# Prompt and decode attention of a hybrid decoder step, run as two stages or as one

## What is computed

```python
def fox_attention(q, k, v, cq, ck, q_pos, k_pos):
    scale = Dh ** -0.5
    ...
        s = jnp.einsum('bqhd,bkhd->bhqk', qi, k).astype(F32) * scale
        s = s + ci[..., None] - ckt[:, :, None, :]
        s = jnp.where(k_pos[None, :] <= pi[:, None], s, MASK_VALUE)
        p = jax.nn.softmax(s, axis=-1).astype(v.dtype)
        return jnp.einsum('bhqk,bkhd->bqhd', p, v)
```

## Time and profile before

| what | us |
|---|---|
| median of three executions | 1936.76 |
| the profiled execution's own time | 1939.86 |
| its span in the profile | 1938.0 |
| TensorE busy in it | 1837.7 |
| last matmul ahead of the attention stages, start | 1021.20 |
| first score of prompt attention, start | 1032.59 |
| first transpose of decode attention, start | 1124.99 |
| first instruction of the next stage (ACT, L1765), start | 1448.45 |

### The profile page before, as it was taken

One profiled execution on the slowest core, in us unless ns is written; L12 is line 12 of the kernel. 1 busy time (PEld: TensorE's weight loads), 2 busy tenths in 40 slices (PEclk: granted clock), 3 DMA queues, 4 the chain that ended last, 5 costly groups with the idle time before them and its releaser, 6 DMA issues. The chain is left out here.

```text
span 1938.0 us, 39358 instructions
## 1 busy us (share of the span) xinstructions
PE 1837.7 (95%) x16353; PEld 1689.5 (87%) x16353; DVE 924.7 (48%) x1392; ACT 692.5 (36%) x1082; POOL 581.1 (30%) x283
## 2 busy tenths in 40 slices
PE   6999998999999999999997999888979999999998
PEld 5999997999999999999995766555559999999998
DVE  4757766345555511156546854343433555555000
ACT  5365454431222212156525754343333322222111
POOL 2333332233333343334325500000003333334332
PEclk9999998999999999999997999999999999999999
DMA  5232241222232323242434799999984222223322
GB/s 120 79 101 79 79 110 40 77 87 87 78 88 77 96 80 86 71 140 55 121 93 112 238 357 380 405 406 407 407 306 122 88 77 88 79 86 89 90 76 79
DMA packets 291653, 277.82 MB, mean 143 GB/s; under 512 B 20114, under 2 KB 250611, under 8 KB 290964
## 3 DMA queue, kind: packets, MB, share of 16 engines
q1 hardware_dynamic: 289540, 272.82, 43.0%
q10 hardware_dynamic: 1792, 1.44, 0.3%
q0 software_dynamic: 144, 1.05, 0.1%
HBM read 254.64 MB, written 16.43 MB: 140 GB/s over the span
## 5 line engine op out<-in xcount | busy, mean ns | idle before, releaser
L2046 POOL TENSOR_TENSOR a_wl<-a_wraw,a_wh 128x1024 fp32r<-128x1024 f32 (+2 forms) x91 | 233.3, 2565 | 394.8 <-ACT a_wh L1970 394.8
L2046 POOL TENSOR_TENSOR b_wl<-b_wraw,b_wh 128x1024 fp32r<-128x1024 f32 (+1 forms) x67 | 175.4, 2618 | 295.1 <-ACT b_wh L1970 295.1
L1927 PE MATMUL ps<-xh,a_wh 128*128 128x288 f32 x1104 | 239.0, 298 | 5.1 <-POOL a_wl L2046 5.1
L1927 PE MATMUL ps<-xl,a_wh 128*128 128x288 f32 x1104 | 237.5, 297 | 0.0
L1927 PE MATMUL ps<-xh,a_wl 128*128 128x288 f32 x1104 | 237.2, 297 | 0.0
L1970 ACT ACTIVATE a_wh<-a_wraw 128x1024 fp32r<-128x1024 f32 (+2 forms) x91 | 100.6, 1105 | 339.5 <-PE ps L1927 324.5
L1970 ACT ACTIVATE b_wh<-b_wraw 128x1024 fp32r<-128x1024 f32 (+1 forms) x67 | 76.0, 1135 | 318.3 <-PE ps L1927 318.3
L1927 PEld LDWEIGHTS ps<-xh,a_wh 128*128 128x128 f32 x1104 | 177.6, 188 | 6.5 <-issue 5.7
L1927 PEld LDWEIGHTS ps<-xh,a_wl 128*128 128x128 f32 x1104 | 177.7, 188 | 0.6
L1927 PEld LDWEIGHTS ps<-xl,a_wh 128*128 128x128 f32 x1104 | 177.7, 188 | 0.6
L2063 DVE TENSOR_TENSOR xT<-xT,ps 128x576 f32<-128x576 f32 x32 | 24.1, 754 | 320.8 <-PE ps L1927 320.8
(11 more groups left out here) (347 smaller groups left out, 3852.7 us busy)
## 6 DMA issues: line engine op xcount, KB each, us to landing
sa_kp<-in_cache_k SPq DMA_DIRECT2D x128, 512.0 KB, 11.2
sa_vp<-in_cache_v SPq DMA_DIRECT2D x82, 512.0 KB, 14.3
a_wraw<-in_w_gate_up SPq DMA_DIRECT2D x44, 512.0 KB, 3.8
b_wraw<-in_w_gate_up SPq DMA_DIRECT2D x44, 512.0 KB, 3.8
a_wraw<-in_a_w_in SPq DMA_DIRECT2D x32, 512.0 KB, 4.2
xT<-in_cache_v SPq DMA_DIRECT2D x28, 512.0 KB, 14.7
a_wraw<-in_w_down SPq DMA_DIRECT2D x16, 704.0 KB, 4.7
b_wraw<-in_w_down SPq DMA_DIRECT2D x16, 704.0 KB, 4.9
```

What stands on the lines that cost most here:

```text
L1927: mm = pe.matmul(ps[0:width(n), bank(n) + a, 0:HALF], wt[:, base(n) + t, 0:width(n)], ap[:, first + t, a * HALF:(a + 1) * HALF], start=kin ...
L2046: pool.tensor_tensor(part(wl, n), part(wraw, n), part(wh, n).bitcast(F32), ALU.subtract).then_inc(e["low"], 1)
```

## The change

`prompt_attention`, `sample_attention`, `KeyPages` and `ValuePages` are replaced by one function, `attention`, and one class, `Pages`.

- All pages, keys and values, go through one ring of 13 places in the order of use: two key pages, then two value pages that are used 22 steps later. Four pages are loaded inside the stage before (at its unit 20), the others from the new stage's start on, each when the page 13 places before it has been used.
- A step handles one page's worth: 128 steps with keys. `key` turns half of two pages' features into two banks (8 transposes), `scores` makes the scores of the step before with four matmuls of 256 columns (512 before), `mix` one value page. Eleven steps at the end have values alone, two pages each.
- The units of prompt attention stand in the steps 8 to 15, 23 to 30 and so on (`FIRST_UNIT` 8, `PAIR_STEPS` 15), one unit a step: score at its step, maximum and exponential one step later, turning two, multiplication four steps later.
- One PSUM bank for prompt scores (four before), one for its output (two), one for the values' output (two), and one ring of three banks for everything turned, of keys, prompt units, probabilities and outputs.
- The split operands of a pair have one buffer; ACT and POOL write both halves themselves, and the DMAs L879 and L881 are gone. Every scaling of a unit is DVE's now. The copies of decode keys and queries into `spare` (L1041 and after) are gone.
- SP issues the mask `c_causal` behind the pages 4 to 12 and the constants of decoding; ACT waits for it (`u["const"]`) at the end of step 1.

The diff, cut to its core:

```diff
-    SCORE_BANKS = (0, 1, 2, 7)
...
-    VPAGES, KGROUPS, KSLOTS, RING = ValuePages.SLOTS, KeyPages.GROUPS, 8, 4
...
+class Pages:
+    HOMES = 13
+    EARLY = 4
+    LAG = 22
...
+            if n < NB * PAGES:
+                self.order += [("k", n), ("k", n + 1)] if n % 2 == 0 else []
+            self.order += [("v", m) for m in self.mixed_at(n)]
...
+    RING, KSLOTS = 3, 4
+    MIX_BANK, UNIT_BANK, OUT_BANK = 5, 6, 7
+    FIRST_UNIT, PAIR_STEPS = 8, 15
+    TURN_LAG, MIX_LAG, OUT_LAG = 2, 4, 11
...
+            for l in range(pages.EARLY, pages.EARLY + 2):
+                page(l)
+            row(0)
+            sp.dma_start(sel[:], k.w["c_rowsel"]).then_inc(e["selloaded"], 16)
+            for l in range(pages.EARLY + 2, pages.EARLY + 6):
+                page(l)
...
+            for l in range(pages.EARLY + 6, pages.HOMES):
+                page(l)
+            row(1)
+            sp.dma_start(causal, k.w["c_causal"]).then_inc(u["const"], 16)
...
+            for n in range(LAST + 2):
+                if n < KSTEPS:
+                    key(n, 0)
+                    key(n, 1)
+                if 1 <= n <= KSTEPS:
+                    scores(n - 1)
+                if mix_at(n) is not None:
+                    unit_mix(mix_at(n))
+                if unit_at(n, TURN_LAG) is not None:
+                    unit_turn(unit_at(n, TURN_LAG))
...
+                for m in pages.mixed_at(n):
+                    mix(m)
...
+                if unit_at(n, 0) is not None:
+                    unit_score(unit_at(n, 0))
...
+            for n in range(LAST + 2):
+                if n < KSTEPS:
+                    key(n)
...
+                if n % 4 == 0 and 4 <= n <= KSTEPS:
+                    save(n // 4 - 1)
...
+                w = unit_at(n, 1)
+                if w is not None:
+                    unit_exponential(w)
...
+                if n == 1:
+                    query_high(0)
+                    act.wait_ge(u["const"], 16)
+        if n == past.PAGES_AT:
+            sp.wait_ge(past.stored, 32)
+            for l in range(Pages.EARLY):
+                self.pages.load(sp, l)
```

More of the change, by code:

```diff
@@ L1586, in _ @@
[L1586 to L1605 removed]
+                mm.then_inc(e["filled"], 1)
@@ new lines, in probabilities, with new_probabilities @@
+            def probabilities(c, g):
+                n = ring["prob", c, g]
+                pe.wait_ge(e["exp"], 3 * c + 2 + g // 2)
+                reuse(n)
+                for p in range(4):
+                    mm = pe.transpose(ring_bank(n)[:, p * P:(p + 1) * P], pr[:, c % 2, (4 * g + p) * P:(4 * g + p + 1) * P], k.ident[:])
+                mm.then_inc(e["filled"], 1)
+            def new_probabilities(c):
+                n = ring["new", c]
+                reuse(n)
+                pe.transpose(ring_bank(n)[0:NQ, 0:P], ptail[:], k.ident[:]).then_inc(e["filled"], 1)
@@ new lines, in _, with key, save, exponentials @@
+        @block.scalar
+        def _(act):
+            def key(n):
+                x = ring["key", n, 0]
+                act.wait_ge(e["filled"], x + 1)
+                if n >= 2:
+                    act.wait_ge(e["scored"], n - 1)
+                act.activation(kt[:, 2 * n % KSLOTS, :], ring_bank(x), ACT.Copy).then_inc(copied["act"], 1)
+            def save(group):
+                b, g = divmod(group, G)
+                act.wait_ge(e["scored"], 4 * group + 4)
+                if b >= 2:
+                    act.wait_ge(e["filled"], ring["prob", b - 2, g] + 1)
+                act.activation(pr[:, b % 2, g * SEQ:(g + 1) * SEQ], ps[:, group % 2, :], ACT.Identity, bias=past.shift[:, b:b + 1]
+                               ).then_inc(e["saved"], 1)
+            def exponentials(c, half):
+                if half == 0:
@@ new lines, in exponentials, with probability @@
+                rows = pr[:, c % 2, half * D:(half + 1) * D]
+                act.activation(rows, rows, ACT.Exp, bias=nm[:, 0:1], accum_out=tot[:, half:half + 1]).then_inc(e["exp"], 1)
+            def probability(c, g):
+                n = ring["prob", c, g]
+                act.wait_ge(e["filled"], n + 1)
+                if c > 0:
+                    act.wait_ge(e["mixed"], (c - 1) * PAGES + 4 * g + 4)
+                act.activation(pp[:, 4 * g:4 * g + 4, :], ring_bank(n).rearrange("p (a n) -> p a n", a=4), ACT.Copy
+                               ).then_inc(copied["act"], 1)
```

1160 lines of the change are left out of this document (508 added, 652 removed).

## The result

The changed kernel took 1943.26 us (median of 20 executions, 1937.74 to 1947.89), the kernel before 1938.74 (20 executions beside them, 1933.08 to 1944.49). The ratio is 1.0029, 95% interval 1.0018 to 1.0039: by the ratio the change costs 5.6 us (3.5 to 7.6; the two medians lie 4.5 apart), at the upper edge of the 0.3% that I had called no change. The forecast was 1.2 us more and 1938.0; the range was 1919 to 1964.

What follows compares the result with a forecast made beforehand. TensorE was taken to bound the merged stage; 1044.5 + (360 - 4.9) + 6.4 + 21.8 + 21.9 = 1449.7 against 1448.45, 1.2 us more, giving a median of 1938.0 us. The range was 1919 to 1964.

Steps and rivals of the forecast that it cites:

- TensorE becomes the bound: Merged attention stage: TensorE work of 357 us against 325 us of page transfers, so TensorE bounds the whole by 30 us.
- ring and early pages: Page loading: the ring of 13 pages and four pages loaded in the projection stage were each costed at nothing.
- the rival of late pages: Plain steps of each period run at 2.58 us instead of 2.0 if SP loses its lead: 16 us, 1954; chance 0.10.
- Smaller pieces: TensorE's changes between transposes and column tiles: 0.27 us paid once in each page, not once in two; 17 us more.
- Waits in the unit steps: TensorE waiting on the one prompt-score bank, for ACT's saves, exponentials and copies, plus small waits: 21.8 us, ends 6.6 and 48.
- the faster rival: Waits in unit steps hide, 6.6 us remaining instead of 21.8: 15 us less, 1923; chance 0.28.
- The start: Stage start: key copies stand behind ACT's wait for the mask, landing at 1043; TensorE goes on at 1044.5.
- The clock: TensorE after the start's idle stretch: 12.7 us at half clock, 6.4 us lost; ends 0 and 8.
- The end: From the last scores to the next stage: the same 21.9 us as before; ends 16 and 28.
- the bank waits of the slower one: Three-bank ring for everything turned too short for half-size steps: 26 us at 0.2 us a step, 1964; chance 0.22.
- the failure that the Trainium skill tells of: TensorE's short waits at banks let the granted clock drop, at 0.96 for 360 us 15 us lost, 1953; chance 0.08.

Runs made afterwards that it cites:

- pairs_save: Changed kernel with value pages paired in odd steps, scores paired in even steps, ACT's save behind the unit's exponential: ratio 0.9953 to the kernel before.
- value_pairs: Changed kernel with two value pages in every odd step instead of one in every step: ratio 1.0035 to the kernel before.
- start_order: Changed kernel with the start's small transfers issued, and ACT's waits for them placed, in order of use: ratio 0.9981 to the kernel before.
- smalls_first: Changed kernel with first decay row, selector, `c_headrow` and mask issued ahead of the stage's first pages: ratio 0.9974 to the kernel before.
- both_parts: Changed kernel with start transfers and waits in order of use, paired values and scores, later save, query copies in step 3: ratio 0.9913 to the kernel before.

## Why the prediction held, and where its steps failed

The stage was forecast 1.2 us longer and is 8.4 longer in the profiles, 5.6 by the timed executions. Time and direction hold. By its own steps, counted from the mark:

- **TensorE becomes the bound**: right. Page waits of the middle are nil. The fall of the transfer rate to 285 to 334 GB/s costs nothing, so ring and early pages go as forecast, and the rival of late pages did not come.
- **Smaller pieces, 17 us**: too small. From 1040.69 to 1421.09 are 380.4 us; less 2.6 for the clock and 6.3 of waits, 371.5 are work, where the sum had 360 - 4.9 = 355.1. The 16.4 more double the term to 33. The price of 0.27 for a change to narrow tiles and back was near; the failed step is the count, "the old order pays 0.27 once in two pages, the new one once in each". That is 64 and 128 groups; the traces have 69 and 205, since a unit's turning or the decay row parts scores and value page in most steps. 33 us over 136 more groups are 0.25 for each, and pairs_save took 0.23 for each group off again.
- **Waits in the unit steps, 21.8 us**: 6.3, about what the faster rival had (6.6). Its time did not come, since the larger work ate it: the errors of 16.4 and 15.5 us cancel nearly. They are linked, for more work covers more of the chain, and value_pairs shows it for 7 us: take work away and the wait comes back. That the whole 15.5 arises this way is not shown, and that the two sizes matched is luck.
- **The start**: I had TensorE go on 21.8 us behind the mark (1044.5 - 1022.66), it was 24.9. The mechanism holds, but the landing was costed by the bytes ahead and came 23.8 us behind the mark instead of 20.3. Only 5.8 us of that lie between its issue and its landing, no more than behind the stores alone (6.4); 17.9 passed before SP issued it. Missed was that the wait for the mask had three others beside it (selector, `c_headrow`, operand rows). Here the Trainium skill (DMA: Bandwidth & Descriptors, "Queues, rings and completion order") says that a queue's descriptors are consumed in ring order on each DMA engine; nothing in these runs speaks against it.
- **The clock, 6.4 us**: 2.6. In the stretch from 1040.69 to 1048.00 it was 0.64 on average, and full behind 1046, with an idle stretch of 8.5 us ahead; before, 12.7 us at half followed 11 us of idle time.
- **The end, 21.9 us**: 29.0, outside my ends by 1 us. The failed step is "I take the same 21.9": twelve pages are issued after the last scores, since their places come free only then, and land 1.29 us apart, and the weights are queued behind them.

Sum of the errors: 3.1 - 3.8 + 16.4 - 15.5 + 7.1 = 7.3 us; with the forecast 1.2 that is 8.5, against 8.4 measured. So the bound and the direction were forecast by reasons that held, and the closeness of the number owes much to errors of both signs. Of the rivals, the bank waits of the slower one did not come at all: key transposes wait for no copy in the middle. The clock kept 1.00 there though banks are cycled every 0.5 us, so the failure that the Trainium skill tells of (TensorE: Matmul & The Clock Gate, "A second HAM failure mode: psum-queue depth-cycling") is not shown by any run here.

## What to carry to other kernels

When two stages are merged to balance two resources, work out the new bound from the start-to-start times of the pieces, each with the neighbour that it will have. Count each change between full-array and narrow matmuls in the order in which a step issues them, with everything that a merged stage puts in between, and not once for each step. Then look at the seam: small transfers queued behind big ones, and waits for them placed earlier on an in-order engine than their data is used, ate here all that the merging gave. A list of such waits has to be made from the program and not from the idle times, since the longest one hides the rest. Where an engine is the bound but a chain on others runs beside it, cut its work and the chain together, so that the steps stay even.

## What the runs showed of the hardware that was not expected

- In the end of the changed kernel TensorE works 0.64 us in every 1.29; from 1439 on the same value page takes 1.08 us, as at 1.2 GHz (the granted clock of the whole end is 0.80), with idle times of 0.2 to 0.65 us between them and none longer since 1426. From 1439.0 to 1445.4 the granted clock is 0.50. In the middle, where waits of up to 1.0 us are rarer, it kept 1.00.
- A wait of 2.0 us ahead of the first unit in start_order was followed by eight transposes in 1.89 us instead of 1.06, as at 1.2 GHz; the same sort of wait in smalls_first, 1.15 us, was not (1.06). In both_parts 3.22 us of waiting there were followed by 0.67 of granted clock over 5.1 us.
- A change from narrow column tiles back to the full array costs 0.12 us whatever the width of the matmuls: four tiles of 256 columns take 0.57 ahead of it and 0.45 ahead of other narrow tiles, four of 512 take 0.99 and 0.88, eight of 256 in a row take 1.00 ahead of it.
